# Seven block products for eight in the merge gates of a two-layer hybrid attention and expert model

## The chip, the cores and the metric

The kernel runs on one core of one Trainium2 chip. The metric is the device time of one execution in microseconds. Engines are named as in the profile: PE is TensorE (matmuls), PEld its weight loads, DVE VectorE, ACT ScalarE, POOL GpSimd, SP SyncE, which issues most DMAs here.

## The reference

All data is float32, 256 tokens of width 1024, two layers. In each layer three attention branches (NSA, MLA, Fox) each give 512 values per token, and a gate merges them:

```python
proj = h @ w_in[l]                      # merge_logits are 3 x 1024 of its columns
gates = sigmoid(merge_logits + b_merge[l]).reshape(B, T, 3, D)
mixed = (gates[:, :, 0] * (out_a @ w_o_nsa[l]) + gates[:, :, 1] * (out_b @ w_o_mla[l])
         + gates[:, :, 2] * (out_c @ w_o_fox[l]))
x = x + mixed @ w_out[l]
x = x + hier_moe(rmsnorm(x, norm_ffn[l]), ...)    # 32 experts, 2 of them per token
```

h is the normed x (256 x 1024). The logits of the gates are thus a product of 256 x 1024 by 1024 x 3072, of the branches 256 x 512 by 512 x 1024 each.

## The kernel before

Each layer has one attention stage and one expert stage. Every engine has its own program in order; semaphores join them.

Weights stream through a ring of slots of 1 MB (`attention_load`, L492). In the attention stage SP issues load n + 8 when the work that used load n is done (L756 to L767). Loads 0 to 12 are columns of `w_in` for projections, load 13 (`L_UQ`) is for the latent queries and keys, loads 14 to 25 (`L_MG`) are the gate weights, 256 columns each, 26 to 31 (`L_WO`) the branch output weights, 32 to 35 (`L_OUT`) those of `w_out`. In between SP also issues the first loads of the expert stage, as their slots come free, and two loads of a bias that depends on distance. In layer 0 alone ScalarE issues one more DMA (L1164), the store of the table of that bias to DRAM: 8 heads x 128 rows x 384 values.

TensorE runs the projections, then the latent queries (L964), keys (L972) and values (L977), the compressed scores (L983), and the transposes of the rotated queries (L993). Then come 16 units, each a branch and a pair of heads. In one unit (L1075 to L1084) TensorE makes the scores of the next unit, one group of gate logits, the transposes of this unit's probabilities, in every third unit one more group of gate logits, and the values of the unit before. The gate logits are the work that fills TensorE while VectorE (`shifted`, `normed`) and ScalarE (`probabilities`, `turned`) make the probabilities. The first two groups stand ahead of the units (L1006, L1073).

A group of gate logits (`gate_logits`, L997) is one block of 128 gate columns for all 256 tokens, transposed: 8 matmuls over the 1024 inputs, the weights stationary, `hT` moving. There are 24 groups a layer. Gate columns lie on partitions, so ScalarE adds the bias as a column and takes tanh in one step (L1205; sigmoid is taken as (1 + tanh(x/2))/2). The bias columns are staged and turned in the setup of the kernel.

After the units the merge (L1087 to L1101) makes 24 blocks of branch outputs, transposed as well, of 4 matmuls each; VectorE multiplies each by its gate plus one (L1490, L1493) and adds (L1497) into `mixT`. The first output projections (`w_out`, L1578) follow at once in `moe_tensor`, and wait for the last blocks of `mixT` one by one (L1586).

In the expert stage each of 8 groups of experts reads 12 loads of 1 MB. 20 slots of the ring and two extra ones are filled ahead; slots come free from the first expert products on (`first_gate_up`, L1678).

Of the kernel before, what the change touches and what calls it, by code (L numbers as in the profile page):

```python
# [15 lines left out]
P = 128  # L16
# [119 lines left out]
def program(nc, A, out, ctx):  # L136
# [49 lines left out]
    mixT = kept(2048, KD, T)  # L186
    oT = kept(4096, 3, 4, T)
    mtmp = kept(7168, 2, T)
# [47 lines left out]
    def gate(q):  # L236

        return region(21504 + T * q, T) if q < 12 else region(18432 + T * (q - 12), T)
# [14 lines left out]
    cols = tiny(0, 118)  # L253
    g_att = tiny(0, DEPTH, KD)
    g_row = tiny(16, DEPTH, KD)
    nbm = tiny(32, DEPTH, 24)
    pecol = tiny(80, DEPTH, 16)
    b1 = tiny(112, 2, DEPTH)
    g_kv = tiny(116, DEPTH, 1)
# [131 lines left out]
    s_mgl = csem("gate_logits_psum")  # L391
# [46 lines left out]
    O_XG, O_WT, O_GU, O_HDT, O_Y, O_SUM = 1, 2, 3, 4, 4, 6  # L438
    nums = [s.num for s in first.values()]
# [131 lines left out]
    def setup_scalar(act):  # L571
# [3 lines left out]
        act.dma_start(stage[32:80, :], A["b_merge"].rearrange("l (c p) -> (l c) p", p=P)).then_inc(u_st, 16)  # L575
        act.dma_start(stage[80:112, :], A["cmp_pe"].rearrange("l (m a) d -> (l m) (a d)", a=2)).then_inc(u_st, 16)
        act.dma_start(stage[112:114, :], A["cmp_k_b1"]).then_inc(u_st, 16)
        act.dma_start(stage[114:116, :], A["cmp_v_b1"]).then_inc(u_st, 16)
        act.dma_start(stage[116:118, :], A["mla_kv_norm"]).then_inc(u_st, 16)
# [35 lines left out]
    def setup_columns_tensor(pe):  # L615
        pe.wait_ge(u_st, 6 * 16)
        pe.transpose(bank[4][:, 0:118], stage[0:118, :], ident[0:118, 0:118]).then_inc(u_prep, 1)
# [16 lines left out]
    def setup_columns_vector(dve):  # L634
        dve.wait_ge(u_prep, 2)
        dve.tensor_copy(cols[:, 16:118], bank[4][:, 16:118]).then_inc(u_cols, 1)
        dve.wait_ge(u_cols, 2)
        dve.tensor_scalar(nbm, nbm, 0.5, None, ALU.mult).then_inc(u_cols, 1)
# [80 lines left out]
    AHEAD = 2  # L719

    CMP_BANK = (6, 5, 4, 2)

    def gate_bank(q):

        return bank[2 + q % 2] if q else bank[7]

    def gates_at(u):

        q = AHEAD + u + (u + 2) // 3
        return q, (q + 1 if u % 3 == 0 else None)  # L730

    for layer in range(DEPTH):
# [13 lines left out]
        def attention_sync(sp):  # L746
# [9 lines left out]
            for n in range(RING, ATT_LOADS):  # L756
                m = n - RING
                if m < L_UQ:
                    sp.wait_ge(s_proj, m + 1)
                elif m == L_UQ:  # L760
                    sp.wait_ge(s_mq, 4)
                    sp.wait_ge(s_mk, 2)
                elif m < L_WO:
                    sp.wait_ge(s_mgl, 2 * (m - L_MG) + 2)
                else:
                    sp.wait_ge(s_mg, 4 * (m - L_WO) + 4)
# [25 lines left out]
                if n == 33:  # L792
# [4 lines left out]
                    sp.wait_ge(s_oe, UNITS)  # L797
                    for c in (6, 7, 8):
                        moe_load(sp, layer, c)

            sp.wait_ge(s_mg, 12)
            moe_load(sp, layer, 10)
            sp.wait_ge(s_mgd, 12)
            moe_load(sp, layer, 15)
            sp.wait_ge(s_mg, 16)
            moe_load(sp, layer, 11)
            sp.wait_ge(s_mgd, 20)
            moe_load(sp, layer, 9)
            sp.wait_ge(s_mg, 20)
            moe_load(sp, layer, 12)  # L810
            sp.wait_ge(s_mg, 24)
            moe_load(sp, layer, 13)
            sp.wait_ge(s_mgd, 24)
            moe_load(sp, layer, 14)
            moe_load(sp, layer, 20)
            for c in range(16, 20):
                sp.wait_ge(s_op, 5 + c - 16)
                moe_load(sp, layer, c)

        def attention_gpsimd(pool):  # L820
# [15 lines left out]
            pool.tensor_tensor(rstd[:, 4:6], ss[:, 0:2], rexp[:, 0:2], ALU.pow).then_inc(s_lrstd, 1)  # L836
            pool.wait_ge(s_wr, 32)
            pool.tensor_tensor(wrt, wrt, bc(g_row[:, layer, :], [P, KD, LW]), ALU.mult).then_inc(s_wrg, 1)

        def attention_tensor(pe):  # L840
# [134 lines left out]
            pe.wait_ge(s_kcT, 1)  # L975
            for t in range(NT):
                pe.matmul(bank[(4, 7)[t]][:, :], ckvT[:, t * P:(t + 1) * P], uv, start=True, stop=True)\  # L977
# [11 lines left out]
            for i in range(4):  # L989
                for a in range(2):  # L990
                    h = 2 * i + a
                    for t in range(NT):
                        last = pe.transpose(bank[i][0:QK, (a * NT + t) * P:(a * NT + t + 1) * P],  # L993
# [3 lines left out]
            def gate_logits(q):  # L997
                if q % 2 == 0:
                    att_wait(pe, L_MG + q // 2)
                if q >= 2:  # L1000
                    pe.wait_ge(s_gt, q - 1)
                wm = slot_cols(L_MG + q // 2, 256)
                columns(gate_bank(q)[:, 0:T], lambda k: wm[:, k, (q % 2) * P:(q % 2 + 1) * P]).then_inc(s_mgl, 1)

            pe.wait_ge(s_mve, 2)
            gate_logits(0)  # L1006
# [66 lines left out]
            gate_logits(1)  # L1073
            pe.wait_ge(s_oce, 4)
            for u in range(UNITS):  # L1075
                before, after = gates_at(u)
                if u + 1 < UNITS:
                    scores(u + 1)
                gate_logits(before)
                turn(u)  # L1080
                if after is not None:
                    gate_logits(after)
# [4 lines left out]
            pe.wait_ge(s_gt, 24)  # L1087
            for q in range(24):
                b, m = BRANCH[q // 8], q % 8
                load = L_WO + q // 4  # L1090
                if q % 4 == 0:
                    att_wait(pe, load)
                if q % 8 == 0:
                    pe.wait_ge(s_oe, (8, 8, UNITS)[q // 8])
                if q >= 4:
# [1051 lines left out]
```

## Time and profile before

| | us |
|---|---|
| median of 3 runs | 1052.14 |
| lowest, highest | 1051.8, 1052.58 |
| profiled execution | 1053.67 |
| its span, first to last instruction | 1051.8 |

Busy share of the span: PE 92%, PEld 67%, DVE 27%, ACT 20%, POOL 2%. The DMA engines moved 292.04 MB. Layer 0's attention stage reaches to about 328 us, its expert stage to about 517 us; layer 1 repeats them some 517.7 us later.

In the profile, a group of instructions is one line of the kernel on one engine with one shape; a float32 matmul of this kernel is recorded as two instructions, a transpose as one. PE's durations overlap, since matmuls are pipelined, so a group's busy time divided by its number of matmuls is what one costs. In a line of idle time, the name behind the arrow is what ended it.

### The profile page before, as it was taken

The page shows a single profiled execution, that of the slowest core. Times are in us where ns is not written, and L with a number is a line of the kernel's source. Part 1 is how long each engine was busy: PE and PEld are TensorE (multiplying, and loading weights), DVE is VectorE, ACT ScalarE, POOL GpSimd, SP SyncE. Part 2 cuts the span into 40 slices and gives each one's busy share as a digit, 9 for nine tenths or more (in the row PEclk, how much of TensorE's full clock was granted, in tenths as well). Part 3 has the DMA queues.
Part 4 walks back from the last instruction along what each step waited for, and adds up shares of the span by engine and source line. Part 5 has one row for each costly group of instructions (what it writes and reads, how often), then busy time and mean ns, then how long its engine had stood idle before and what let it go on. Part 6 is the DMA issues. An engine that isn't in the chain of part 4 may idle for free. (4 is left out here: it accounts for less than half of the span.)

```text
span 1051.8 us, 14177 instructions
## 1 busy us (share of the span) xinstructions
PE 968.3 (92%) x5804; PEld 699.7 (67%) x5804; DVE 280.5 (27%) x961; ACT 215.2 (20%) x576; POOL 25.3 (2%) x72
## 2 busy tenths in 40 slices
PE   9999999999999996786899999999999999976675
PEld 8888788778887543333288887887888855522341
DVE  2321533442423111110130215344333331100112
ACT  1211354550012020000111015544400302000001
POOL 0000000000000000000010000000000000000000
PEclk9999999999999998888999999999999999988898
DMA  9956663528956999999997452543299489999995
GB/s 298 331 180 194 113 194 99 187 84 262 378 199 267 422 421 420 422 421 421 358 322 246 161 160 86 161 160 121 81 344 374 161 347 421 420 422 420 421 417 190
DMA packets 134871, 292.04 MB, mean 278 GB/s; under 512 B 13838, under 2 KB 101140, under 8 KB 113044
## 3 DMA queue, kind: packets, MB, share of 16 engines
q1 hardware_dynamic: 131440, 288.36, 74.2%
q10 hardware_dynamic: 3364, 2.74, 1.6%
q8 instruction: 47, 0.77, 0.3%
q14 instruction: 20, 0.16, 0.0%
HBM read 288.44 MB, written 2.64 MB: 277 GB/s over the span
## 5 line engine op out<-in xcount | busy, mean ns | idle before, releaser
L856 PE MATMUL bank<-tail,ring 128*128 128x256 f32 x1280 | 289.1, 382 | 0.0
L856 PEld LDWEIGHTS bank<-tail,ring 128*128 128x128 f32 x1280 | 239.2, 190 | 39.4 <-issue 8.7
L1667 PE MATMUL bank<-ring,tail 128*32 128x512 f32 x896 | 115.7, 675 | 53.0 <-DMA ring<-in_moe_w_up 49.0
L1667 PEld LDWEIGHTS bank<-ring,tail 128*32 128x32 f32 x896 | 32.8, 122 | 133.0 <-issue 133.0
L1099 PE MATMUL bank<-tail,ring 128*128 128x256 f32 x384 | 83.4, 380 | 0.0
L1099 PEld LDWEIGHTS bank<-tail,ring 128*128 128x128 f32 x384 | 72.8, 190 | 10.2 <-issue 0.3
L1946 DVE SCALAR_TENSOR_TENSOR tail<-tail,bank 128x256 f32<-128x256 f32 x16 | 6.7, 420 | 264.7 <-ACT tail L1802 264.7
L1196 ACT ACTIVATE ring<-ring,small 128x128 f32<-128x128 f32 (+1 forms) x128 | 56.6, 443 | 75.0 <-DVE small L1443 75.0
L1716 PE MATMUL bank<-ring,tail 128*32 128x512 f32 x480 | 58.6, 596 | 7.1 <-DMA ring<-in_moe_w_down 4.2
L1674 PE MATMUL bank<-tail 128*128 128x512 f32 x128 | 59.2, 605 | 0.0
L1587 PE MATMUL bank<-ring,tail 128*128 128x256 f32 x256 | 56.9, 380 | 0.0
L862 PE MATMUL bank<-ring,tail 128*128 128x256 f32 (+2 forms) x320 | 53.6, 327 | 0.0
L1638 PEld LDWEIGHTS bank<-tail 128*128 128x128 f32 x384 | 45.2, 196 | 11.3 <-issue 10.6
L1802 ACT ACTIVATE tail<-bank 128x256 f32<-128x256 f32 x16 | 6.1, 383 | 227.1 <-PE bank L1667 205.7
L1587 PEld LDWEIGHTS bank<-ring,tail 128*128 128x128 f32 x256 | 48.2, 190 | 6.3
L862 PEld LDWEIGHTS bank<-ring,tail 128*128 128x128 f32 x320 | 49.6, 191 | 3.5
L1638 PE MATMUL bank<-tail 128*128 128x128 f32 x384 | 47.9, 284 | 2.5 <-ACT tail L1785 2.0
L1674 PEld LDWEIGHTS bank<-tail 128*128 128x128 f32 x128 | 23.0, 189 | 36.4 <-issue 36.4
L1436 DVE CUSTOM_DVE_ANT_0 ring<-bank,ring 128x128 f32<-128x128 f32 x96 | 28.6, 354 | 50.4 <-PE bank L1040 50.1
L1716 PEld LDWEIGHTS bank<-ring,tail 128*32 128x32 f32 x480 | 14.6, 109 | 35.8 <-issue 24.3
L1040 PE MATMUL bank<-ring 64*128 64x128 f32 (+3 forms) x256 | 34.8, 347 | 0.0
L1458 DVE TENSOR_TENSOR ring<-ring,small 128x256 f32<-128x256 f32 x64 | 32.8, 554 | 1.1
(277 smaller groups left out, 837.5 us busy)
## 6 DMA issues: line engine op xcount, KB each, us to landing
ring<-in_moe_w_up SPq DMA_DIRECT2D x56, 1024.0 KB, 24.4
ring<-in_moe_w_gate SPq DMA_DIRECT2D x56, 1024.0 KB, 22.3
ring<-in_moe_w_down SPq DMA_DIRECT2D x52, 1024.0 KB, 16.1
ring<-in_w_in SPq DMA_DIRECT2D x48, 1024.0 KB, 7.8
ring<-in_moe_w_gate SPq DMA_DIRECT2D x16, 512.0 KB, 8.5
ring<-in_moe_w_up SPq DMA_DIRECT2D x16, 512.0 KB, 8.9
ring<-in_w_out SPq DMA_DIRECT2D x8, 1024.0 KB, 8.3
ring<-in_moe_w_down SPq DMA_DIRECT2D x16, 512.0 KB, 16.1
```

The costliest lines, as they stand in the source:

```text
L856: last = pe.matmul(dst, weight(k), hT[:, k, :], start=(k == 0), stop=(k == KD - 1))
L862: last = pe.matmul(dst, tokens[:, k, t * P:(t + 1) * P], weight(k), start=(k == 0), stop=(k == KD - 1))
L1040: last = pe.matmul(bank[half][:, lo:hi], q[:, t * P:(t + 1) * P], k[:, 0:hi - lo], start=True, stop=True)
L1099: last = pe.matmul(bank[q % 4][:, 0:T], wo[:, c, (m % 4) * P:(m % 4 + 1) * P], oT[:, b, c, :], start=(c == 0), stop=(c == 3))
L1196: last = act.activation(pr, pr, ACT.Exp, scale=scale, bias=mx[:, c:c + 1], accum_out=sm[:, c:c + 1])
L1436: last = dve.tensor_tensor_reduce(out=prob[u % 3][:, half, lo:hi], in0=bank[half][:, lo:hi], in1=b, scale=1.0, scalar=PAD, op0=ALU.add, op ...
L1458: last = dve.tensor_tensor(pr, pr, bc(factors(rs, u)[:, t, :], [P, 2, hi - lo]), ALU.mult)
L1587: last = pe.matmul(bank[4 + i][:, t * T:(t + 1) * T], mixT[:, k, t * P:(t + 1) * P], w[:, k, :], start=(k == 0), stop=(k == KD - 1))
L1638: last = pe.matmul(b[:, (k % 4) * P:(k % 4 + 1) * P], rows_k, Sel[:, g % 2, t, :], start=(t == 0 and k % 4 == 0), stop=(t == NT - 1), skip ...
L1667: last = pe.matmul(bank[4][CAP * e:CAP * e + CAP, :].rearrange("p (a f) -> p a f", a=2), XT[:, k, CAP * e:CAP * e + CAP], ring[:, lo:lo + ...
L1674: return pe.matmul(bank[2 * t + half][:, :], ST[:, t * P:(t + 1) * P], ysb[:, 512 * half:512 * half + 512], start=(g == 0), stop=(g == NGR ...
L1716: last = pe.matmul(bank[5 + n][CAP * e:CAP * e + CAP, :], hidden_rows(g)[:, a, CAP * e:CAP * e + CAP], moe_home(place(g, 8 + e))[:, a * D ...
```

## The change

Two gate weight loads now form a pair (left and right, 256 columns each, 6 pairs a layer). The product of tokens by the weights of a pair is a 2 x 2 by 2 x 2 product of blocks (tokens in halves of 128, inputs in halves of 512, columns in halves of 256). It is made by Winograd's form with seven block products instead of eight. The sums of token blocks (`hsum`) are made once a layer, the differences of weight blocks in place in the ring slots, four a pair, all on GpSimd. Each block product is 4 matmuls with tokens stationary and 256 weight columns moving, so gates now lie by rows: tokens on partitions. The partial sums of a pair are built in three PSUM banks, which ScalarE seeds (the bias, spread over the partitions by a DMA, or an earlier product) before matmuls add to them; two of the four quarters get a last addition on VectorE. `ORDER` gives the order of the 42 pieces; two stand in each unit where one group stood, one more in every third unit, and four ahead of the units.

The merge is by rows too: 12 steps of 4 matmuls of 512 columns. The merged rows are turned back by 16 transposes (`turn_mixed`), copied to `mixT` by ScalarE, and the first four output projections are made in two halves. Attention values use one PSUM bank instead of two. The staging of bias columns leaves the setup.

```diff
@@ SP, attention_sync
                 elif m == L_UQ:
                     sp.wait_ge(s_mq, 4)
+                    for p in range(2):
+                        sp.dma_start(gbias[p], bias_row(layer, p)).then_inc(s_gb[p], 16)
                     sp.wait_ge(s_mk, 2)
                 elif m < L_WO:
-                    sp.wait_ge(s_mgl, 2 * (m - L_MG) + 2)
+                    sp.wait_ge(s_gp, product(4, (m - L_MG) // 2))
                 else:
-                    sp.wait_ge(s_mg, 4 * (m - L_WO) + 4)
+                    sp.wait_ge(s_mg, 2 * (m - L_WO) + 2)
+    ORDER = [(1, 0), (5, 0), (2, 0), (3, 0)]
+    for p_ in range(1, PAIRS):
+        ORDER += [(1, p_), (6, p_ - 1), (5, p_), (2, p_), (7, p_ - 1), (3, p_), (4, p_ - 1)]
+    ORDER += [(6, PAIRS - 1), (7, PAIRS - 1), (4, PAIRS - 1)]
+    def bias_row(layer, p):
+        at = BRANCH[p // 2] * D + 512 * (p % 2)
+        return A["b_merge"][layer, at:at + 512].partition_broadcast(P)
@@ GpSimd, attention_gpsimd
+            pool.tensor_tensor(hsum[:, 0], a21, a22, ALU.add).then_inc(s_hs, 1)
...
+            first_difference(0)
+            bias_difference(0)
+            first_difference(1)
+            bias_difference(1)
+            for p in range(PAIRS):
+                (left_top, left_bottom), (right_top, right_bottom) = halves(p, 0), halves(p, 1)
+                pool.wait_ge(s_gp, product(3, p))
+                pool.wait_ge(s_tp, difference(1, p))
+                pool.tensor_tensor(right_bottom, right_bottom, right_top, ALU.subtract).then_inc(s_tp, 1)
+                pool.wait_ge(s_gp, product(1, p))
+                pool.wait_ge(s_tp, difference(2, p))
+                pool.tensor_tensor(left_top, right_bottom, left_top, ALU.subtract).then_inc(s_tp, 1)
+                pool.wait_ge(s_gp, product(2, p))
+                pool.tensor_tensor(left_bottom, left_bottom, right_bottom, ALU.subtract).then_inc(s_tp, 1)
+                if p + 2 < PAIRS:
+                    first_difference(p + 2)
+                    bias_difference(p + 2)
@@ TensorE, attention_tensor
-            def gate_logits(q):
...
+            def gate_piece(kind, p):
+                left, right = slot_cols(L_MG + 2 * p, 256), slot_cols(L_MG + 2 * p + 1, 256)
+                if kind == 1:
+                    att_wait(pe, L_MG + 2 * p)
+                    pe.wait_ge(s_seed, seeded("left", p))
+                    block_product(psum_left, hT[:, 0:4, 0:P], left[:, 0:4]).then_inc(s_gp, 1)
+                elif kind == 5:
+                    pe.wait_ge(s_hs, 4)
+                    pe.wait_ge(s_tp, difference(1, p))
+                    pe.wait_ge(s_seed, seeded("right", p))
+                    block_product(psum_right, hsum[:, 0], right[:, 0:4]).then_inc(s_gp, 1)
...
+                elif kind == 7:
+                    pe.wait_ge(s_tp, difference(3, p))
+                    pe.wait_ge(s_u, 2 * p + 1)
+                    block_product(psum_common, hsum[:, 2], left[:, 0:4]).then_inc(s_gp, 1)
...
-            pe.wait_ge(s_mve, 2)
-            gate_logits(0)
+            gate_piece(1, 0)
+            gate_piece(5, 0)
             pe.wait_ge(s_mqte, 4)
             pe.wait_ge(s_pc, 1)
...
                 pe.wait_ge(s_pta, u + 1)
-                if u >= 2:
-                    pe.wait_ge(s_oe, u - 1)
-                o = bank[6 + u % 2]
+                if u >= 1:
+                    pe.wait_ge(s_oe, u)
+                o = bank[6]
...
-            for q in range(24):
+            for j in range(2 * PAIRS):
...
                 for c in range(4):
-                    last = pe.matmul(bank[q % 4][:, 0:T], wo[:, c, (m % 4) * P:(m % 4 + 1) * P],
-                                     oT[:, b, c, :], start=(c == 0), stop=(c == 3))
+                    last = pe.matmul(bank[j % 4][:, :], oT[:, b, c, t * P:(t + 1) * P], wo[:, c, :],
+                                     start=(c == 0), stop=(c == 3))
                 last.then_inc(s_mg, 1)
+                if j >= 2 * PAIRS - 3:
+                    turn_mixed(pe, j - 9)
@@ ScalarE, attention_scalar, behind the copies of the latent values
+            def seed_left(p):
+                act.wait_ge(s_gb[p % 2], 16 * (p // 2 + 1))
+                if p == 0:
+                    act.wait_ge(s_mve, 2)
+                else:
+                    act.wait_ge(s_gt, tanh_done(2, p - 1))
+                act.activation(psum_left, gbias[p % 2][:, 0:T], ACT.Copy).then_inc(s_seed, 1)
...
+            seed_left(0)
+            seed_right(0)
             act.wait_ge(s_sx, 1)
             act.activation(pc, pc, ACT.Exp, scale=0.125).then_inc(s_sexp, 1)
...
+                elif kind == 6:
+                    act.wait_ge(s_u, 2 * p + 1)
+                    act.activation(tile[:, 0, T:2 * T], tile[:, 0, T:2 * T], ACT.Tanh, scale=0.5).then_inc(s_gt, 1)
@@ VectorE, attention_vector
+                if kind == 6:
+                    dve.wait_ge(s_gp, product(6, p))
+                    dve.wait_ge(s_cp, 3 * p + 3)
...
+                    dve.tensor_tensor(tile[:, 0, T:2 * T], psum_common, right53, ALU.add).then_inc(s_u, 1)
```

## Rows read from the trace of the kernel before

**Rows 1.** The page, busy time and share of the span by engine.
```profile
PE 968.3 (92%) x5804; PEld 699.7 (67%) x5804; DVE 280.5 (27%) x961; ACT 215.2 (20%) x576; POOL 25.3 (2%) x72
```
**Rows 2.** Waits of PE, longest in total: us, times, longest.
```profile
PE bank L1667 <- DMA ring<-in_moe_w_up: 49.0, 6, 8.8
```
**Rows 3.** Windows: length, busy us of five engines, PE clock, DMA share, GB/s.
```profile
300.00:350.00 50.00, 48.47 (x299) 37.42 (x298) 17.19 (x70) 11.11 (x23) 3.38 (x10) 0.97 0.64 253
350.00:400.00 50.00, 49.40 (x349) 23.20 (x347) 5.92 (x14) 8.01 (x10) 1.52 (x4) 1.00 1.01 421
```
**Rows 4.** Groups by shape: busy us, mean ns of one, idle before.
```profile
L856 PE MATMUL bank<-tail,ring 128*128 128x256 f32 x1280 | 289.1, 382 | 0.0
L1099 PE MATMUL bank<-tail,ring 128*128 128x256 f32 x384 | 83.4, 380 | 0.0
L1674 PE MATMUL bank<-tail 128*128 128x512 f32 x128 | 59.2, 605 | 0.0
L1051 PE MATMUL bank<-cst,ring 128*128 128x128 f32 x192 | 26.2, 273 | 0.0
L1205 ACT ACTIVATE ring<-bank,small 128x256 f32<-128x256 f32 x48 | 22.4, 472 | 46.3 <-PE bank L856 46.3
```
**Rows 5.** Timeline of PE, layer 0: start us, length us.
```profile
107.68 5.32 PE L964 MATMUL bank<-ring 128*128 128x384 f32 x16
...
119.97 3.62 PE L856 MATMUL bank<-tail,ring 128*128 128x256 f32 x16
...
129.74 3.72 PE L856 MATMUL bank<-tail,ring 128*128 128x256 f32 x16
133.30 0.82 PE L1051 MATMUL bank<-cst,ring 128*128 128x128 f32 x6
133.96 3.62 PE L856 MATMUL bank<-tail,ring 128*128 128x256 f32 x16
```
**Rows 6.** Groups of POOL by shape.
```profile
L1571 POOL TENSOR_TENSOR tail<-tail,small 128x128 f32<-128x128 f32 x32 | 12.1, 400 | 330.9 <-PE bank L1696 308.6 <-DVE small L1935 22.2
L838 POOL TENSOR_TENSOR tail<-tail,small 128x320 f32<-128x320 f32 x2 | 1.5, 753 | 267.2 <-DMA tail<-in_moe_w_router 267.2
```
**Rows 7.** Timeline of all engines in one unit of layer 0.
```profile
141.81 0.18 DVE L1449 RECIPROCAL small<-small 128x4 f32<-128x4 f32 x1 [1.93 <-ACT ring L1196]
...
147.88 0.82 PE L1051 MATMUL bank<-cst,ring 128*128 128x128 f32 x6
```
**Rows 8.** Timeline in the expert stage: a VectorE copy and the matmuls behind it.
```profile
343.60 0.42 DVE L1959 COPY tail<-bank 128x256 f32<-128x256 f32 x1 [1.44 <-PE bank L1702]
...
344.07 0.16 PEld L1716 LDWEIGHTS bank<-ring,tail 128*32 128x32 f32 x8 [0.54 <-DVE tail L1959]
```
**Rows 9.** Timelines of DMA issues, ScalarE's and SP's: start, length to the last's end.
```profile
100.98 0.79 ACTq L1164 DMA_DIRECT2D bias_table<-tail  x1
107.87 7.30 SPq L497 DMA_DIRECT2D ring<-in_w_in  x2
...
625.59 7.31 SPq L497 DMA_DIRECT2D ring<-in_w_in  x2
```
**Rows 10.** DMA in windows 106:110, 134:135 and 624:628: issue to landing, packets by queue.
```profile
ring<-in_w_in SPq DMA_DIRECT2D x1, 1024.0 KB, 27.4
...
q10 hardware_dynamic: 9, 0.00, 1.8%
...
ring<-in_w_in SPq DMA_DIRECT2D x1, 1024.0 KB, 5.3
```
**Rows 11.** Windows in the expert stage, columns as in rows 3.
```profile
413.00:416.00 3.00, 0.00 (x0) 0.00 (x0) 0.00 (x0) 0.00 (x0) 0.00 (x0) 0.71 1.00 418
...
422.00:425.00 3.00, 3.00 (x21) 0.82 (x17) 0.00 (x0) 0.00 (x0) 0.00 (x0) 0.58 1.00 418
```
**Rows 12.** Timeline of PE in the expert stage.
```profile
392.91 7.07 PE L1667 MATMUL bank<-ring,tail 128*32 128x512 f32 x64
...
419.49 9.55 PE L1667 MATMUL bank<-ring,tail 128*32 128x512 f32 x64 [7.72 <-DMA ring<-in_moe_w_up]
```

More of the change, by code:

```diff
@@ L615, in setup_columns_tensor @@
     def setup_columns_tensor(pe):
[L616 to L617 removed]
+        pe.wait_ge(u_st, 5 * 16)
+        pe.transpose(bank[4][:, 0:70], stage[0:70, :], ident[0:70, 0:70]).then_inc(u_prep, 1)
     def setup_bias_tensor(pe):
@@ L818, in attention_sync, with turn_mixed @@
                 moe_load(sp, layer, c)
+        def turn_mixed(pe, i):
+            n, t = divmod(i, 2)
+            pe.wait_ge(s_mgd, 2 * PAIRS - 4 + i + 1)
+            for a in range(4):
+                last = pe.transpose(bank[i][:, a * P:(a + 1) * P],
+                                    mix[:, t, (4 * n + a) * P:(4 * n + a + 1) * P], ident)
+            last.then_inc(s_mxt, 1)
         def attention_gpsimd(pool):
@@ L975, in attention_tensor @@
             pe.wait_ge(s_kcT, 1)
+            pe.wait_ge(s_mqe, 3)
             for t in range(NT):
-                pe.matmul(bank[(4, 7)[t]][:, :], ckvT[:, t * P:(t + 1) * P], uv, start=True, stop=True)\
+                pe.matmul(bank[MV_BANK[t]][:, :], ckvT[:, t * P:(t + 1) * P], uv, start=True, stop=True)\
                   .then_inc(s_mv, 1)
@@ L1216, in attention_scalar @@
             probabilities(0)
-            for q in range(AHEAD):
-                gate_tanh(q)
+            gate_step(2, 0)
+            gate_step(3, 0)
             for u in range(UNITS):
-                before, after = gates_at(u)
+                before, after = pieces_at(u)
                 if u + 1 < UNITS:
                     probabilities(u + 1)
-                gate_tanh(before)
+                for kind, p in before:
+                    gate_step(kind, p)
                 turned(u)
-                if after is not None:
-                    gate_tanh(after)
+                for kind, p in after:
+                    gate_step(kind, p)
+            for i in range(4):
+                n, t = divmod(i, 2)
+                act.wait_ge(s_mxt, i + 1)
+                act.activation(mixT[:, 4 * n:4 * n + 4, t * P:(t + 1) * P],
+                               bank[i][:, :].rearrange("p (k c) -> p k c", k=4), ACT.Copy).then_inc(s_mxe, 1)
         def attention_vector(dve):
@@ L1603, in moe_tensor @@
             for i in range(4):
-                w_out(0, i)
+                w_out(0, i, range(0, 4))
+                if i == 3:
+                    turn_mixed(pe, 3)
+            for i in range(4):
+                w_out(0, i, range(4, 8))
             w_out(1, 0)
```

282 lines of the change are left out of this document (201 added, 81 removed).

## The prediction

> **What bounds the kernel now.** I read the page's busy times first: TensorE is busy 92% of the span [rows 1]. Then its waits: the longest, 49.0 us, is for expert weights in the mixture-of-experts part (MoE) [rows 2]; in the attention part it hardly waits at all. The windows place this. Between 300 and 350 us DMA is at 0.64, so the slots that can be filled ahead are full; from 350 on it is at 1.01 and 421 GB/s [rows 3]. That stream starts when the first expert products free their slots. So the MoE part is a block of fixed length behind the moment at which TensorE reaches it, and whatever TensorE gains or loses before it moves the end one for one, in both layers. That leaves TensorE's own order of work in attention: what it executes, and what is late for it.
>
> **Gate products.** Before: 24 groups of 8 matmuls (128x128 against 256 columns) a layer. After: 6 pairs x 7 products x 4 = 168 matmuls of the same size. The trace counts each such matmul as two instructions, so L1099 took 83.4/192 = 0.434 us each and L856 289.1/640 = 0.452 [rows 4]; inside the units one group of 8 and what follows it took 133.30 - 129.74 = 3.56 us [rows 5], 0.445 each with its edge. I take 0.434: 24 fewer x 0.434 = 10.4 us less a layer (bounds 10.4 to 10.8).
>
> **Merge.** 96 matmuls of 256 columns become 48 of 512. Twice 0.434 is 0.87 us; L1674, which is 512 wide, took 59.2/64 = 0.925, some of it at the low clock [rows 4]. So between 0 and 48 x 0.057 = +2.7 us a layer; I take 0, the columns being the same. Added are 16 transposes a layer, one instruction each: 26.2/192 = 0.136 us [rows 4], six of them in 133.96 - 133.30 = 0.66 [rows 5]. 16 x 0.136 + a little for edges = 2.3 us a layer (1.8 to 3). Their evictions to SBUF (ScalarE, 4 of 512 columns) and VectorE's two steps per half row lie beside 3.5 us of matmuls each; the split of the first output projection puts 16 matmuls (7 us) between the third and fourth block of transposes and what needs them. I cost them at nothing. Without that cover one eviction would cost about 1 us.
>
> **Added steps beside the units.** ScalarE had four tanh of 0.472 us [rows 4] per pair; it now has ten steps, some 4.2 us for 1.9. VectorE gets two additions of 0.42 (the size of its copy in rows 8). A pair takes three units, some 20 us. The cover: VectorE starts scaling the probabilities of a unit at 141.81 and the transposes that want them start at 147.88 [rows 7]; with 1.24 us for it, 4.8 us are free. A new wait of ScalarE for VectorE's sum (about 0.9 us) sits ahead of the eviction of the transposes, which is wanted a unit later. Nothing is late in the middle of the stage.
> Two places are bare. In unit 15 products 6 and 7 of the last pair follow each other and share a PSUM bank, so 7 waits for the sum of 6; and the values of unit 15 now wait until those of unit 14 are taken from the one remaining bank. One such turn through VectorE is shown by L1959 to L1716: TensorE's weight load idle 0.54 us [rows 8]. With the shorter wait of product 4: 2 x 0.54 + 0.2 = 1.3 us a layer (0.8 to 2). At the start, product 1 of pair 1 waits for a seed that ScalarE writes after the first unit's exponentials: 0.3 us (0 to 1).
>
> **GpSimd.** It is not measured at this size. Its in-SBUF multiplies took 400 ns for 128 and 753 ns for 320 elements [rows 6]: 1.84 ns an element and 0.16 fixed, so 2.05 us for 1024 (proportional to 753: 2.4). Four a pair and one of 256 make 8.8 us in 20. The tightest use is product 6: after product 3 frees the slot, TensorE has product 4, transposes, values, scores and the next product 1 ahead, about 6 us for one difference of 2.05. Cost 0 (up to 1 us a layer).
> The Trainium skill ("SBUF — State Buffer", Who interferes with whom) says that a VectorE instruction with two SBUF inputs and a GpSimd one that reads SBUF lock each other out for the whole instruction. No row of before shows such a pair for long. By that rule each scaling could be late by one difference, 2.05 us, which the 4.8 us swallow, and the sum would stay.
> Sum so far, each layer: -10.4 + 0 + 2.3 + 1.3 + 0.3 = -6.5 us.
>
> **The bias rows in layer 0.** This is where I think the change loses. The gate bias no longer comes through ScalarE's bias operand: ScalarE copies 128 identical rows of it into PSUM ahead of products 1 and 5, and SP issues these rows (2 x 256 KB) only after the last latent q product (L964 ends at 107.68 + 5.32 = 113.0 us [rows 5]). TensorE wants the first gate product at 119.97 [rows 5]. Seven us would be ample, and in layer 1 it is: there the load ahead of them is issued at 625.59 [rows 9] and lands 5.3 us later [rows 10]. In layer 0, however, ScalarE has issued the store of the bias table (1.5 MB) at 100.98 [rows 9], and the load that SP issues at 107.87 (the first of the two in that row) lands 27.4 us later [rows 10], at 135.3. The ScalarE queue still has its last 9 packets between 134 and 135 [rows 10]. In the kernel before that load is a gate slot for much later, so nobody sees it. The bias rows are issued 5 us behind it on the same queue, and a landing counts only when every DMA engine is done; on the engines that serve the table they come after that load. 256 KB at the 421 GB/s of rows 3 are 0.6 us; I put them at 135.3 + 0.7 = 136.0 (bounds: 135.3, and 139.7, where the next load after them lands).
> Waiting for them is not TensorE alone: ScalarE is in order, so behind its seed stand the exponentials of the compressed scores and the copies of q, and SP's later loads. With 0.5 us for the copy into PSUM and the signal, product 1 starts at 136.5: 136.5 - 119.97 = 16.5 us of stall (15.5 to 20).
> The clock adds to it. When TensorE waited 7.7 us before 419.49, the granted clock fell to 0.5 (1.2 GHz) in the fourth us of idleness and was still there three us after work resumed [rows 11]; the same 64 products took 9.55 us after it and 7.07 before [rows 12]. So +2.5 us (1.5 to 4).
> Layer 0: -6.8 (the 0.3 of the start lies inside the stall) + 16.5 + 2.5 = +12.2. Layer 1: -6.5. Together +5.7 us. From the profiled execution, 1053.67 us (span 1051.80): 1059.4. That one is 1.5 us over the median of the runs, 1052.14; on the median the same sum gives **1057.8 us**.
>
> **Rivals.**
> (a) The bias rows come in time, since they are small and the fast half of the engines carries them. Then layer 0 gains as layer 1 does: -6.5 x 2 = -13, 1039.1. For it: the rows are a quarter of a load, and another order among the engines than I assume would bring them early; against: the load issued just ahead of them on the same queue took 27.4 us. 14%.
> (b) They come ahead of the load's rest on the slow engines, at 124 to 131: stall 4.5 to 11.5 and the clock, total -8 to +1: about 1048. 9%.
> (c) Slower still: besides the stall, GpSimd or the port bites. If a difference took over 6 us, product 6 would wait in each pair; if it took over 4.8 us, GpSimd would be the engine that sets the pair's 20 us. Half a us of wait at two products in each of the 12 pairs would be 12 us on top: 1070. For it: an unmeasured size, in-order waits of ScalarE on VectorE inside each unit; against: rows 6 and 7. 15%.
> (d) The change doing less than it says: the merges at 0.925 (+5.4 in two layers) and the transposes at the upper bound, 1063. This is in the forecast's range.
> The forecast itself has 62%.
>
> **Numbers.** 0.2% of 1052 is 2.1 us, about what can be told from no change. Faster (under 1050): (a) and most of (b), with little from the forecast: 0.19. Same: 0.07. Slower: 0.74. The range: the terms' bounds about the forecast give 1053 to 1064; taking in the upper part of (b) and the lower of (c) it is 1048 to 1066, leaving (a) and the rest of (c) out.
>
> **What would show it.** Right: in the new trace TensorE is idle for about 16 us from 120 us on, until a DMA of the bias rows and ScalarE's copy behind it; the granted clock falls there; the same place in layer 1 shows no wait; the units stage (first gate product to last) is about 9 us shorter in both layers; the merge unchanged in length; GpSimd subtractions near 2.05 us. Wrong: no idle stretch at 120 us (then a); waits of TensorE in products 6, 7 or 4 with GpSimd or VectorE as releasers all through the units (then c); an MoE part that does not move with its start.

## The result, and the profile after

| | before | after |
|---|---|---|
| median of the runs, us | 1051.97 (4 runs) | 1063.62 (4 runs) |
| lowest to highest, us | 1051.13 to 1052.58 | 1062.99 to 1065.24 |
| profiled execution, span, us | 1053.67, 1051.80 | 1064.25, 1062.5 |

The ratio is 1.0103, 95% interval 1.0089 to 1.0118: the change made the kernel 11.65 us slower. The forecast was 1057.8, between 1048 and 1066. The profiled executions stand 10.6 us apart, and the sums below are made against those.

The page of the changed kernel, answering to [rows 1]:

```profile
PE 953.6 (90%) x5548; PEld 650.5 (61%) x5548; DVE 341.4 (32%) x944; ACT 233.6 (22%) x656; POOL 163.8 (15%) x140
```

TensorE executes 256 matmul records fewer and 15 us less, and yet the end is later. So time stands between its instructions. The waits of PE (us, times, longest) say where:

```profile
PE bank L1895 <- DMA ring<-in_moe_w_up: 52.2, 6, 9.6
PE bank L1097 <- ACT bank L1312: 16.7, 2, 16.3
...
PE bank L1097 <- DVE ring L1686: 2.8, 2, 1.4
...
PE bank L1191 <- DVE tail L1676: 1.2, 2, 0.6
...
PE bank L1097 <- ACT ring L1346: 0.9, 1, 0.9
PE bank L1177 <- DVE ring L1660: 0.6, 1, 0.6
```

The first line was there before, at 49.0 [rows 2]; the stretch of the kernel around it is as long as before, as the balance below shows. L1097 is a block product, L1312 ScalarE's copy of the bias rows into PSUM: one wait of 16.3 us. PE's timeline of layer 0 places it, ScalarE's timeline says what it waited for, and the DMA view of the window 104 to 118 gives issue to landing (last column, us):

```profile
108.19 5.32 PE L1060 MATMUL bank<-ring 128*128 128x384 f32 x16
...
118.71 1.93 PE L1090 MATMUL bank<-cst,ring 128*96 128x128 f32 x16
136.92 6.55 PE L1097 MATMUL bank<-ring,tail 128*128 128x256 f32 x16 [16.28 <-ACT bank L1312]
```
```profile
136.39 0.39 ACT L1312 ACTIVATE bank<-ring 128x256 f32<-128x256 f32 x1 [18.43 <-DMA ring<-in_b_merge]
```
```profile
ring<-in_w_in SPq DMA_DIRECT2D x1, 1024.0 KB, 27.3
ring<-in_b_merge SPq DMA_DIRECT2D x2, 256.0 KB, 22.9
```

Before, the first gate product began at 119.97 [rows 5]. Now it begins at 136.92, and the two products there take 6.55 us for 3.62, because the clock is low. Windows of the changed kernel (columns as in [rows 3], the PE clock third from the end):

```profile
122.00:125.00 3.00, 0.00 (x0) 0.00 (x0) 0.00 (x0) 0.00 (x0) 0.00 (x0) 1.00 0.65 108
125.00:128.00 3.00, 0.00 (x0) 0.00 (x0) 0.00 (x0) 0.00 (x0) 0.00 (x0) 0.61 0.92 224
128.00:131.00 3.00, 0.00 (x0) 0.00 (x0) 0.00 (x0) 0.00 (x0) 0.00 (x0) 0.50 0.52 82
...
139.00:142.00 3.00, 3.00 (x8) 2.37 (x8) 2.97 (x6) 1.23 (x3) 1.28 (x2) 0.50 0.09 20
142.00:144.00 2.00, 2.00 (x13) 1.52 (x14) 1.97 (x2) 0.49 (x2) 0.00 (x0) 0.82 0.51 122
```

In layer 1 the same place has no wait: the product starts right behind the transposes.

```profile
649.11 1.93 PE L1090 MATMUL bank<-cst,ring 128*96 128x128 f32 x16
650.88 3.62 PE L1097 MATMUL bank<-ring,tail 128*128 128x256 f32 x16
```

The groups by shape, answering to [rows 4] and [rows 6]; L1660 is VectorE's scaling of the probabilities, L1645 the small scaling of four row maxima, L924 one of GpSimd's four differences of weights:

```profile
L1097 PE MATMUL bank<-ring,tail 128*128 128x256 f32 x672 | 159.4, 389 | 20.5 <-ACT bank L1312 16.7 <-DVE ring L1686 2.8 <-ACT ring L1346 0.9
L1228 PE MATMUL bank<-ring,tail 128*128 128x512 f32 x192 | 83.6, 593 | 0.0
```
```profile
L1660 DVE TENSOR_TENSOR ring<-ring,small 128x512 f32<-128x512 f32 x32 | 49.9, 1558 | 0.0
L1645 DVE TENSOR_SCALAR small<-small 128x4 f32<-128x4 f32 x32 | 16.3, 509 | 1.1
```
```profile
L924 POOL TENSOR_TENSOR ring<-ring 128x1024 f32<-128x1024 f32 x12 | 28.6, 2385 | 108.7 <-PE bank L1097 108.7
```

A merge matmul of 512 columns costs 83.6/96 = 0.871 us. VectorE's two lines were 683 and 170 ns before, in the kernel without GpSimd's differences:

```profile
L1458 DVE TENSOR_TENSOR ring<-ring,small 128x512 f32<-128x512 f32 x32 | 21.9, 683 | 0.0
...
L1443 DVE TENSOR_SCALAR small<-small 128x4 f32<-128x4 f32 x32 | 5.4, 170 | 1.1
```

The balance, from the starts of the first gate product, the first merge product and the first expert product of each layer in PE's timelines:

| stretch | before, us | after, us | difference |
|---|---|---|---|
| start to first gate product, layer 0 | 119.97 | 136.92 | +16.95 |
| units, layer 0 | 125.87 | 122.04 | -3.83 (-6.77, and +2.94 of low clock) |
| merge to first expert product, layer 0 | 82.60 | 82.50 | -0.10 |
| expert part of layer 0 to units of layer 1 | 309.25 | 309.42 | +0.17 |
| units, layer 1 | 125.87 | 120.41 | -5.46 |
| merge to first expert product, layer 1 | 80.98 | 84.00 | +3.02 |
| from there to the end | 207.3 | 207.2 | -0.1 |

The sum is +10.6. In each of the two executions the clock dipped once where the tokens are gathered behind the merge: the same 16 instructions took 3.37 us for 2.02 in layer 0 of the kernel before, 3.20 for 2.02 in layer 1 of the one after. From the first merge product to these instructions, where neither dip counts, TensorE took 75.87 us before and 77.39 after: the merge stretch is 1.5 us longer in each layer.

### The profile page after: what moved, and what is told of

Read it like the earlier page. It is cut to its first block and busy times, and to the rows that moved or that the text cites. A ratio compares the mean times of both kernels' runs of the same rounds, so it can differ in the third digit from the quotient of the medians.

```text
span 1062.5 us, 13935 instructions
## 1 busy us (share of the span) xinstructions
PE 953.6 (90%) x5548; PEld 650.5 (61%) x5548; DVE 341.4 (32%) x944; ACT 233.6 (22%) x656; POOL 163.8 (15%) x140
## 5 line engine op out<-in xcount | busy, mean ns | idle before, releaser
L1097 PE MATMUL bank<-ring,tail 128*128 128x256 f32 x672 | 159.4, 389 | 20.5 <-ACT bank L1312 16.7
L1097 PEld LDWEIGHTS bank<-ring,tail 128*128 128x128 f32 x672 | 126.2, 193 | 46.6 <-issue 27.1
L1895 PEld LDWEIGHTS bank<-ring,tail 128*32 128x32 f32 x896 | 32.2, 121 | 134.0 <-issue 134.0
L952 PE MATMUL bank<-tail,ring 128*128 128x256 f32 x512 | 112.8, 380 | 0.0
L952 PEld LDWEIGHTS bank<-tail,ring 128*128 128x128 f32 x512 | 96.5, 190 | 13.2 <-issue 0.4
L1228 PE MATMUL bank<-ring,tail 128*128 128x512 f32 x192 | 83.6, 593 | 0.0
L1660 DVE TENSOR_TENSOR ring<-ring,small 128x256 f32<-128x256 f32 x64 | 67.3, 1092 | 1.1
L1794 POOL TENSOR_TENSOR tail<-tail,small 128x128 f32<-128x128 f32 x32 | 12.1, 400 | 332.8 <-PE bank L1924 310.7
L1228 PEld LDWEIGHTS bank<-ring,tail 128*128 128x128 f32 x192 | 36.0, 190 | 43.4 <-issue 43.4
L1810 PE MATMUL bank<-ring,tail 128*128 128x256 f32 x256 | 57.2, 380 | 0.0
L1866 PEld LDWEIGHTS bank<-tail 128*128 128x128 f32 x384 | 45.0, 196 | 11.1 <-issue 10.6
L958 PEld LDWEIGHTS bank<-ring,tail 128*128 128x128 f32 x320 | 49.6, 191 | 3.5
L1810 PEld LDWEIGHTS bank<-ring,tail 128*128 128x128 f32 x256 | 47.9, 190 | 6.1
L924 POOL TENSOR_TENSOR ring<-ring 128x1024 f32<-128x1024 f32 x12 | 28.6, 2385 | 108.7 <-PE bank L1097 108.7
```

The costliest lines, as they stand in the source:

```text
L924: pool.tensor_tensor(right_bottom, right_bottom, right_top, ALU.subtract).then_inc(s_tp, 1)
L952: last = pe.matmul(dst, weight(k), hT[:, k, :], start=(k == 0), stop=(k == KD - 1))
L958: last = pe.matmul(dst, tokens[:, k, t * P:(t + 1) * P], weight(k), start=(k == 0), stop=(k == KD - 1))
L1097: last = pe.matmul(dst, tokens[:, k, :], weights[:, k, :], start=False, stop=(k == KD // 2 - 1), skip_group_check=True)
L1228: last = pe.matmul(bank[j % 4][:, :], oT[:, b, c, t * P:(t + 1) * P], wo[:, c, :], start=(c == 0), stop=(c == 3))
L1660: last = dve.tensor_tensor(pr, pr, bc(factors(rs, u)[:, t, :], [P, 2, hi - lo]), ALU.mult)
```

## Experiments

The theory: the loss is the 16.4 us of stall and the 2.9 us of low clock behind it, both from the table's store; everything else of the change gains, though less than forecast, since GpSimd's differences hold VectorE. The first four experiments ran beside runs of the kernel before with a median of 1052.64 us, the next four beside others with 1052.46, the last two beside others with 1053.12; each ratio is against the runs beside it.

**The store issued later, in the changed kernel.** ScalarE issues it behind its copies of q.

```diff
-            if layer == 0:
-                act.wait_ge(u_cp, 1)
-                act.dma_start(table, tabs.unsqueeze(1).broadcast_to([H, P, OH_W])).then_inc(u_tb, 16)
             for i in range(2):
@@ behind the copies of q
+            if layer == 0:
+                act.wait_ge(u_cp, 1)
+                act.dma_start(table, tabs.unsqueeze(1).broadcast_to([H, P, OH_W])).then_inc(u_tb, 16)
```

> ScalarE issues the store of the bias table of layer 0 only after its copies of q, behind both seeds. Theory (the bias rows stand behind that store and the load ahead of them): the wait of 16.3 us before the first gate product of layer 0 and the slow clock after it (the first two products took 6.4 us for 3.45) go, and the first gate product starts near 120.5 us as in the kernel before: 1063.6 - 16.4 - 2.9 = 1044.3 us, 7.7 us under the kernel before. Rival (the rows are slow of themselves, being one row read 128 times, or the store stands in the way wherever it is): at least 4 us of the wait stay, or as much comes up later in the units; 1050 or more.

Measured: 1053.28 us (before 1052.64), ratio 1.0006, interval 0.9994 to 1.0019. The 16 us are gone, but not all of the time came back: the theory's 1044.3 is missed by 9 us, and the rival's second form, that as much comes up later, is what happened. ScalarE's timeline, then PE's:

```profile
121.27 0.79 ACTq L1338 DMA_DIRECT2D bias_table<-tail  x1
...
122.87 7.93 ACTq L1349 DMA_DIRECT2D ring<-in_b_merge  x1
...
130.85 0.38 ACT L1354 ACTIVATE ring<-bank 128x256 f32<-128x256 f32 x1 [6.97 <-issue]
```
```profile
120.94 3.62 PE L1097 MATMUL bank<-ring,tail 128*128 128x256 f32 x16
...
131.56 1.24 PE L1143 MATMUL bank<-ring 32*128 32x256 f32 x8 [5.93 <-ACT ring L1386]
```

The first gate product starts at 120.94, without a wait. But ScalarE's next DMA issue, the bias row of pair 2, took 7.93 us right behind the store on ScalarE's own queue, where such an issue otherwise takes 0.35; all that ScalarE does behind it was late, TensorE waited 5.93 us, and the clock fell again. The store moved its price to another engine.

**The same move in the kernel before.**

> The kernel before with the same move of the store. Theory: there the late load is a gate slot that nobody wants yet, so the move gives nothing: 1052.0 within 1 us. Rival (the store slows the attention stage of layer 0 in itself, and e1's gain is not about the bias rows): 1049 or less.

Measured: 1053.02 us, ratio 1.0001, interval 0.9989 to 1.0014; the first gate product at 120.07. Without the bias rows the store costs nothing in either place. So the loss belongs to the change together with the store.

**TensorE kept busy through the wait.** 64 matmuls on an idle bank ahead of the first gate product of layer 0.

```diff
+            if layer == 0:
+                keep_warm(pe, 64, bank[6])
             gate_piece(1, 0)
```

> The changed kernel with 64 matmuls of 128 columns, whose result nobody reads, in the wait of layer 0 ahead of the first gate product. They take about 64 x 0.243 = 15.6 us and end before the bias rows are there. Theory (the idle engine's clock fell, and the first products ran at 1.2 GHz for it): the wait is filled, the granted clock stays at 1.0, the first two products take 3.5 us: 1063.6 - 2.9 = 1060.7. Rival (the products were slow for their operands or for GpSimd's traffic): they still take over 6 us and the time stays at 1063.6.

Measured: 1062.85 us, ratio 1.0092, interval 1.0074 to 1.0109. This separates little:

```profile
120.55 14.46 PE L573 MATMUL bank<-cst 128*128 128x128 f32 x128
138.45 5.38 PE L1097 MATMUL bank<-ring,tail 128*128 128x256 f32 x16 [3.44 <-ACT bank L1314]
```

The filler ended at 135.0 and the rows came 1.5 us later than in the changed kernel, so TensorE was idle for 3.44 us; the window 138 to 140 shows a clock of 0.68 and 140 to 142 one of 0.50. The products took 5.38 us for 6.55. This filler ended too early to keep the clock for the work behind it.

**The bias rows issued ahead of the load.** SP holds the 1 MB load at 107.87 until the rows are issued.

```diff
+                    if m == L_UQ - 1:
+                        sp.wait_ge(s_mq, 4)
+                        for p in range(2):
+                            sp.dma_start(gbias[p], bias_row(layer, p)).then_inc(s_gb[p], 16)
                 elif m == L_UQ:
-                    sp.wait_ge(s_mq, 4)
-                    for p in range(2):
-                        sp.dma_start(gbias[p], bias_row(layer, p)).then_inc(s_gb[p], 16)
```

> SP holds the seventh gate load until the bias rows are issued, so that in layer 0 nothing stands ahead of them on SP's queue; the store goes on beside them. Theory as forecast (the rows wait for the rest of the load ahead of them on the engines that also serve the store): with the load gone the rows come at 122 to 126 us, the wait shrinks from 16.3 to 2 to 6 us, 1049 to 1054. Rival (the store itself holds them, whatever stands ahead on the queue): they land near 134 to 135, the wait is 14 us or more, 1061 to 1063.

Measured: 1057.43 us, ratio 1.0049, interval 1.0032 to 1.0065.

```profile
131.13 5.52 PE L1098 MATMUL bank<-ring,tail 128*128 128x256 f32 x16 [10.51 <-ACT bank L1313]
```

Issued at 113.57 with nothing of SP's ahead of them, the rows still took 18.0 us for 256 KB. So the load ahead accounts for some 6 us of the stall. The other 10 are the store's, as the next experiment shows: with the store out of the way the same rows in the same place landed in 3.4 us. This falls between what theory and rival named: I had the rows queued behind the load, and most of their delay is the store itself.

**The store issued in unit 0.** As in the first experiment, but behind ScalarE's steps of unit 0, where its next DMA issue is a few units away.

```diff
                     gate_step(kind, p)
+                if layer == 0 and u == 0:
+                    act.wait_ge(u_cp, 1)
+                    act.dma_start(table, tabs.unsqueeze(1).broadcast_to([H, P, OH_W])).then_inc(u_tb, 16)
```

> The changed kernel with one thing moved: ScalarE issues the store of the bias table behind its steps of unit 0 of layer 0, so neither the load of latent v nor the bias rows of the first units are behind it. Theory (of the 11.65 us that the change costs, 16.4 are the wait for the bias rows and 2.9 the cold clock behind it): the first gate product starts at 120 to 121, no ScalarE step waits 6 us for its own queue, and the time is 1063.6 - 16.4 - 2.9 = 1044.3. Rival 1 (the store holds whatever is beside it, wherever it is put): the wait turns up again at a later load, the stored bias row of a later unit or the weights of a half, with 5 to 10 us, and the time is 1050 to 1054, as with the store behind the copies of q. Rival 2 (GpSimd's differences are what costs): merges and units take as long as in the changed kernel and the time is above 1052.

Measured: 1045.3 us (before 1052.46), ratio 0.9932, interval 0.9912 to 0.9951.

```profile
118.67 1.93 PE L1090 MATMUL bank<-cst,ring 128*96 128x128 f32 x16
120.44 3.62 PE L1097 MATMUL bank<-ring,tail 128*128 128x256 f32 x16
```

The DMA view of the window 111 to 119 has the bias rows of layer 0, issued at 113.50:

```profile
ring<-in_b_merge SPq DMA_DIRECT2D x2, 256.0 KB, 3.4
```

So the rows are not slow of themselves, which was a rival of the first experiment. Moving these lines turned 11.65 us of loss into 7.2 us of gain; the theory said 1044.3. The store is issued at 137.79 and neither it nor anything beside it holds TensorE. The units take 120.4 us in both layers. ScalarE's next DMA issue, at 155.18, took 0.33 us.

**GpSimd's differences over 4 columns of 1024.** It leaves out nearly all of the weight differences; instructions, waits and products are the same.

```diff
-                pool.tensor_tensor(right_top, right_top, left_top, ALU.subtract).then_inc(s_tp, 1)
+                pool.tensor_tensor(right_top[:, 0:4], right_top[:, 0:4], left_top[:, 0:4], ALU.subtract).then_inc(s_tp, 1)
...
```

> As the kernel with the store in unit 0, but each difference of weights on GpSimd covers 4 columns of its 1024, so it leaves out nearly all of them, and the merged result is another. Same instructions, waits and products. Theory (GpSimd's long operations hold VectorE): the row scaling of 128x512 on VectorE goes back from 1558 ns to near 683, the small one of 128x4 from 509 to near 170, the wait at the first turned unit of layer 1 (0.6) and the 1.4 before the last unit's product 7 are gone, and the time is 2 to 4 us under the kernel with the store in unit 0. Rival (VectorE's longer steps lie off the path, and the waits at the end of the units come from their order alone): less than 1 us.

Measured: 1040.05 us, 5.3 under the kernel with the store in unit 0; ratio 0.9872, interval 0.9853 to 0.9891. VectorE's groups:

```profile
L1660 DVE TENSOR_TENSOR ring<-ring,small 128x512 f32<-128x512 f32 x32 | 21.9, 683 | 0.0
...
L1645 DVE TENSOR_SCALAR small<-small 128x4 f32<-128x4 f32 x32 | 5.4, 170 | 1.1
```

The units take 117.5 us in both layers, 2.9 less: that is what GpSimd's differences cost a layer, through VectorE. It was more than the 2 to 4 us in all that I had expected. TensorE waits for GpSimd itself nowhere in the units, with whole differences or short ones, so the shorter differences did not help it directly. Not all of the 5.8 us reaches the end. In the profiled executions the span is 3.5 us shorter: 1.1 us came back in the expert part of layer 0 and 1.5 in that of layer 1; over both, TensorE's waits for the down weights grew from 2.6 to 5.9 us. By the medians 0.5 came back. One execution says little here: the stretch from the first expert product of layer 0 to the units of layer 1 took from 309.0 to 310.8 us over all the profiled executions, and the 310.8 is the kernel before with its store moved.

**The last unit in another order.** Product 6, the turn, product 7, the values of unit 14, product 4, the values of unit 15.

```diff
+        if u == UNITS - 1:
+            return ORDER[n:n + 1], ORDER[n + 1:n + 3]
@@ TensorE, behind turn(u)
+                if u == UNITS - 1:
+                    gate_piece(*after[0])
+                    values(u - 1)
+                    gate_piece(*after[1])
+                    continue
```

> As the kernel with the store in unit 0, with the last unit's steps on TensorE in another order: product 6, the turn of the rows, product 7, values of unit 14, product 4, values of unit 15; so the last product isn't behind a sum of VectorE's. Theory (the end of the units costs 2.6 us a layer because product 7 waits 1.4 for VectorE's sum and the last values 0.6 for its copy): 1 to 2 us less a layer, 2 to 4 in all. Rival (the wait moves to the product behind the turn, since VectorE is late there, not out of order): within 0.5 us of the kernel with the store in unit 0.

Measured: 1043.08 us, 2.2 under the kernel with the store in unit 0; ratio 0.9911, interval 0.9893 to 0.9929. PE's timeline at the end of the units, first with the store in unit 0, then in the new order:

```profile
230.72 1.99 PE L1097 MATMUL bank<-ring,tail 128*128 128x256 f32 x8
234.09 1.97 PE L1097 MATMUL bank<-ring,tail 128*128 128x256 f32 x8 [1.38 <-DVE ring L1686]
...
240.04 0.65 PE L1191 MATMUL bank<-ring 128*64 128x256 f32 x4 [0.61 <-DVE tail L1676]
```
```profile
230.61 1.99 PE L1099 MATMUL bank<-ring,tail 128*128 128x256 f32 x8
233.23 0.88 PE L1179 MATMUL bank<-cst,ring 128*128 128x128 f32 x6 [0.63 <-DVE ring L1667]
```

Both waits are gone and one of 0.63 has come: theory and rival each have a part. The units take 119.1 us, 1.3 less a layer.

**The small scaling on ScalarE**, on top of the new order.

```diff
-                dve.tensor_scalar(m, m, -scale, None, ALU.mult).then_inc(s_max, 1)
@@ ScalarE, ahead of its exponentials
+                s(act.activation(m, m, ACT.Copy, scale=-scale))
+                s.sync()
...
```

With the scaling VectorE also loses the `s.sync()` ahead of it, in which it waited for its own four maxima; ScalarE now waits for them. The run does not separate the two.

> As the kernel with the last unit reordered, and the small scaling of the row maxima (128x4) done by ScalarE instead of VectorE, where it took 0.51 us on average and 2.14 once beside a difference of GpSimd's. Theory (VectorE is held by GpSimd, ScalarE is not): VectorE's row scalings start earlier, the wait of the second unit of layer 0 (0.54) is gone, 0.5 to 1 us in all. Rival (ScalarE has become the engine behind the turned units, with the steps it already does): ScalarE's step of some 0.2 us and its wait stand ahead of every exponential, 32 times, and the time is 1 to 3 us above the kernel with the last unit reordered.

Measured: 1040.92 us, 2.2 less again; ratio 0.9885, interval 0.9867 to 0.9904. The units take 118.2 us, 0.9 less a layer, more than the theory's 0.5 to 1 us for both layers. The two waits of TensorE for ScalarE, 0.5 and 0.9 us early in each layer's units, are gone, and one for VectorE's scaling grew from 0.4 or 0.5 to 0.9; and the rival's price for 32 more steps on ScalarE doesn't appear.

**Each difference in two operations of 512 columns**, on top of that.

```diff
+            def difference_in_two(out, a, b):
+                pool.tensor_tensor(out[:, 0:2 * T], a[:, 0:2 * T], b[:, 0:2 * T], ALU.subtract)
+                pool.tensor_tensor(out[:, 2 * T:], a[:, 2 * T:], b[:, 2 * T:], ALU.subtract).then_inc(s_tp, 1)
...
```

> As the kernel with the last unit reordered and the small scaling on ScalarE, but each difference of weights on GpSimd is made by two operations of 512 columns. Theory (an operation on VectorE that falls beside one of GpSimd's waits for the end of that one operation): the longest row scaling on VectorE falls from 2.85 us to about 2.0 (half a difference is some 1.3 us, of 2.36 for a whole one and 0.20 for one of 4 columns), its mean over 128x512 from 1575 ns to 1000 to 1300, the units of a layer get 0.3 to 1 us shorter, the time 0.5 to 2 us. Rival (GpSimd and VectorE share the time by halves, or VectorE waits until GpSimd has nothing left): the mean and the longest stay, and GpSimd's added 0.2 us per difference leaves the time the same or up to 1 us above.

Measured: 1040.05 us (before 1053.12), ratio 0.9874, interval 0.9847 to 0.9901. Its scalings, and one line of GpSimd:

```profile
L1670 DVE TENSOR_TENSOR ring<-ring,small 128x512 f32<-128x512 f32 x32 | 43.3, 1353 | 0.0
...
L1670 DVE TENSOR_TENSOR ring<-ring,small 128x256 f32<-128x256 f32 x32 | 21.4, 669 | 1.1
```
```profile
L908 POOL TENSOR_TENSOR ring<-ring 128x512 f32<-128x512 f32 x48 | 63.7, 1328 | 172.4 <-PE bank L1103 97.5 <-DMA ring<-in_w_in 73.1
```

The longest scaling fell from 2.85 us to 1.76, and the units to 116.6 us, 1.6 less a layer. That is the theory, and against the rival; the mean fell only to 1353 ns, above the 1000 to 1300 expected, the halves costing GpSimd 2.7 us for 2.4. The one wait left for TensorE in the units of each layer is of 0.2 us, for GpSimd. As times, this kernel and the one before it can't be told apart (the intervals overlap); the stretch of the units can. Of the kernels that leave nothing out it has the lowest ratio.

**Differences over 4 columns again**, on the kernel with the small scaling on ScalarE; it leaves out nearly all of them.

> As the kernel with the last unit reordered and the small scaling on ScalarE, but each difference on GpSimd covers 4 of its 1024 columns, so it leaves out nearly all of them. Theory (the reordering and the moved scaling took away part of the 2.9 us a layer that GpSimd's long operations cost): the units of a layer take 0.5 to 1.5 us less than with whole differences, the time is 1 to 3 us less, 1038 to 1040. Rival (the two edits took away other waits, and contention still costs 2.9 a layer): 5 to 6 us less, 1035 to 1036.

Measured: 1037.53 us, ratio 0.9856, interval 0.9828 to 0.9884; the units take 116.2 us in both layers. So GpSimd cost 2.0 us a layer there, for 2.9 in the kernel with the store in unit 0: more than the 0.5 to 1.5 expected, and less than the rival's 2.9. Of the 2.2 us that the two edits saved a layer, 0.9 were contention, and 1.3 come without GpSimd's long operations too. Halving the differences takes back 1.6 of the 2.0.

## Why the prediction was nearly right, point by point

**The bias rows (right, to 0.1 us of stall).** Forecast: product 1 at 136.5, a stall of 16.5 us. Measured: 136.92, of which 0.5 are an earlier delay, and 16.4. The fifth experiment shows the cause: with the store out of the way the start is 120.44. The reason that I gave for the size was less than half of it, so that the size came out this well is luck. I had the rows landing behind the load issued ahead of them. By that mechanism the fourth experiment should have left a wait of 2 to 6 us; with that load behind them the rows still took 18.0 us, and 10.5 us of wait stayed.

The Trainium skill ("DMA: Bandwidth & Descriptors", Issuing engines are not separate DMA queues) says that DMAs issued by different engines run on the same 16 DMA engines and interleave. The trace agrees: a store on ScalarE's queue made 256 KB on SP's take 18.0 to 22.9 us, for 5.3 in layer 1 and 3.4 in layer 0 with the store moved.

**The clock (right).** Forecast +2.5 us, measured 2.9, with the granted clock at 0.50 for the first products. A small misreading: the clock of [rows 11] fell in the third us of idleness, not the fourth. In the changed kernel it fell some 5 us into the idleness, and with the filler only after work had resumed.

**Gates (right as a sum, once contention is out).** Forecast: -10.4 + 1.3 + 0.3 = -8.8 us between the first gate product and the merge; I had named some 9 us in both layers as a sign of being right, and the changed kernel shows 6.8 and 5.5. With the contention taken away the stretch fell from 125.87 to 117.5, -8.4. The last experiment, where TensorE waits for nothing in the units, has 116.2: the products alone gave 9.7, for 10.4.

**GpSimd (the step that failed).** I costed it at 0 (up to 1 us a layer), on two grounds. One was that a difference takes 2.05 us; it took 2.39 to 2.75 on average by line of the kernel, and the 2.4 that I had put in brackets was the nearer. The other was that the 4.8 us ahead of the transposes swallow one difference. For most units they do: in layer 1 of the changed kernel TensorE waits three times within 20 us of the first gate product (0.42, 0.56 and 0.95 us), then for nothing until the last unit. But four differences can run back to back, so VectorE is held more than once in a unit. From layer 1 of the changed kernel, VectorE and GpSimd:

```profile
660.50 4.84 DVE L1660 TENSOR_TENSOR ring<-ring,small 128x256 f32<-128x256 f32 x2
```
```profile
659.95 2.35 POOL L924 TENSOR_TENSOR ring<-ring 128x1024 f32<-128x1024 f32 x1 [7.56 <-PE bank L1097]
662.44 2.35 POOL L927 TENSOR_TENSOR ring<-ring 128x1024 f32<-128x1024 f32 x1
```

The first line holds two scalings, which take 1.1 us together undisturbed (0.42 and 0.68); here TensorE waited 0.56 us for the second. And in the last unit no slack stands before the sum that product 7 waits for. Price by the sixth experiment: 2.9 us a layer; in the changed kernel some 1.3 of layer 0's fell into the stall. Rival (c) had named this mechanism; its price, 12 us in all, was far above the 4.5 that were left.

The Trainium skill ("SBUF — State Buffer", Who interferes with whom) says that whoever issues first keeps the shared port pair for the whole instruction, and that a tensor_scalar can enter a two-port mode, in which it needs the pair too. The runs agree with both: halved operations cut the longest wait, and the 128x4 scaling took 509 ns on average for 170, once 2.14 us, from 165.13 to the end of a difference at 167.24. I had drawn from this page only that a scaling is late by one difference.

**End of the units (mis-sized, by contention).** Forecast 1.3 us a layer, measured 2.0: 1.38 for product 7 and 0.62 for the last values. The 0.54 of [rows 8] was a wait for a VectorE that was idle; here VectorE was still scaling. Of the 2.0, 0.8 is contention, counted above (the two waits for the sum fell from 2.8 to 1.2 us in the sixth experiment); the 1.2 that are left are close to the forecast.

**Merge and transposes (mis-sized, the other way).** Forecast 0 + 2.3 us, measured 1.5. A merge matmul took 0.861 us inside its run and a block of four transposes held up the matmuls by 0.43 us, less than the 0.54 that I took.

**The sum.** Forecast +5.7, measured +10.6 between the profiled executions: 5.6 us less gained in the units, 0.4 more of low clock, 0.5 at the start, 1.6 less lost in the merge (dips aside). The direction was right because the stall was. That the expert part only moves with its start held to 0.2 us here; in the later kernels up to 1.5 us came back in it. Two sums of the forecast are off: rival (d) adds 5.4 and 1.4 to 1057.8, which is 1064.6, not 1063, and the upper bounds of all terms give 1074, not 1064. The measured time lies near the upper end of the range mostly because of the contention.

**What the forecast did not draw out** is that the loss is separable: rival (a) gave 1039.1 for rows in time, the kernel with the store in unit 0 took 1045.3, and with the three further edits the change reaches 1040.05.

Left open: why the store slows SP's DMAs by that much (the DMA share stood at 0.51 to 0.52 from 128 to 136.5 us, as if half the engines were at work, but no run changed how the store is spread), and why the merge stretch has dips of the clock in some executions.

## What to carry to other kernels

When a change adds a small load that the path needs, look at what is in flight on every DMA queue at that moment, not only on its own; here a store of 1.5 MB made 256 KB take 18 to 23 us, and moving it was free where nobody needed it soon and its issuing engine had no further DMA to issue for 17 us. Put long GpSimd operations where VectorE is idle, or cut them, and count how many of them come back to back, since slack for one is not slack for several. When a change that should gain loses, take away the one large wait first: what is left tells you the worth of the rest.

## What the runs showed of the hardware that I had not expected

- A DMA issue on ScalarE took 7.93 us when it followed the 1.5 MB store on the same queue by 1.6 us; it takes 0.35 otherwise. SP, on the other queue, was held too: in the changed kernel its issue of the second bias row took 5.55 us, and with the store in unit 0 both rows were issued in 0.82. An issue is not always free for its engine.
- GpSimd's subtraction of 128x1024 took 2.39 to 2.75 us (means by line of the kernel; 2.35 at its shortest), of 128x512 1.33 to 1.41, of 128x4 0.20 to 0.27.
- A 128x4 operation of VectorE took 2.14 us beside GpSimd's difference, and never more than 0.17 with differences of 4 columns.
